# Splitting the normalised rows with the norm's weights alone, and applying the reciprocal root where products leave PSUM

## What is computed

```python
def rms_norm(x, g):
    x32 = x.astype(jnp.float32)
    y = x32 * lax.rsqrt(jnp.mean(x32 * x32, axis=-1, keepdims=True) + EPS)
    return (y * g.astype(jnp.float32)).astype(x.dtype)

def swiglu_ffn(h, w_gate_up, w_down):
    gate, up = jnp.split(h @ w_gate_up, 2, axis=-1)
    return (jax.nn.silu(gate) * up) @ w_down
...
        x = x + y
        x = x + swiglu_ffn(rms_norm(x, norm_ffn[i]), w_gate_up[i], w_down[i])
...
    kv = rms_norm(x, norm_kv) @ w_kv
...
    s = jnp.einsum('...qkgd,...ckd->...kgqc', q, k, preferred_element_type=jnp.float32) * ATTN_SCALE
```

## Time and profile before

| | us |
|---|---|
| median of 3 runs (3222.97 to 3225.34) | 3224.47 |
| the profiled execution | 3223.44 |
| its span, first to last instruction | 3221.6 |
| PE matmul busy | 3057.3 |
| DVE busy | 1764.2 |
| ACT busy | 1380.2 |
| POOL busy | 244.7 |

### The profile page before, as it was taken

The page is one execution under the profiler, slowest core; times in us unless marked ns, Lnnn a source line. Parts: engine busy times, 40 slices in busy tenths (PEclk is TensorE's granted clock), DMA queues, the critical chain, the costliest instruction groups (busy, mean ns, idle before and its releaser), DMA issues.

```text
span 3221.6 us, 72232 instructions
## 1 busy us (share of the span) xinstructions
PE 3057.3 (95%) x27157; PEld 2946.7 (91%) x27157; DVE 1764.2 (55%) x2676; ACT 1380.2 (43%) x2035; POOL 244.7 (8%) x295
## 2 busy tenths in 40 slices
PE   5899999999999998999999999879989999999998
PEld 3899999999998898999999999868888999999997
DVE  2577677677676545544444444556545444444444
ACT  3455455454454333444444333345534444443333
POOL 0111111111121001100000000120002000000000
PEclk8999999999999999999999999989999999999999
DMA  7545545545544454555555555534345555555553
GB/s 212 152 136 161 150 137 160 148 140 155 150 143 151 154 173 148 166 181 180 179 181 177 177 174 177 162 115 132 112 150 157 179 179 181 178 182 175 179 172 130
DMA packets 514689, 519.06 MB, mean 161 GB/s; under 512 B 30876, under 2 KB 437541, under 8 KB 513893
## 3 DMA queue, kind: packets, MB, share of 16 engines
q1 hardware_dynamic: 505490, 498.85, 50.0%
q0 software_dynamic: 2128, 13.69, 1.3%
q10 hardware_dynamic: 6866, 3.50, 0.4%
HBM read 491.99 MB, written 32.82 MB: 163 GB/s over the span
## 4 chain that ended last, share of the span: by engine, by line
PE 86%; DVE 7%; issue 3%; ACT 2%; DMA 1%; SPq 0%; DVEq 0%; ACTq 0%; POOLq 0%
PE bank L442 26%; PE bank L443 24%; PE bank L444 24%; PE bank L1619 4%; DVE norm_h L579 1%; DVE s_dec L2079 1%; DVE w_lo L430 1%; DVE h_lo L595 1%; ACT w_hi L423 1%; PE bank L1757 0%; PE bank L1804 0%; PE bank L1646 0%; DVE x_res L2125 0%; DMA hcol<-in_dt_bias_dram 0%; PE bank L962 0%
## 5 line engine op out<-in xcount | busy, mean ns | idle before, releaser
L430 DVE TENSOR_TENSOR w_lo<-w_raw,w_hi 128x1024 fp32r<-128x1024 f32 x830 | 1015.0, 1224 | 1042.8 <-ACT w_hi L423 1042.5
L423 ACT ACTIVATE w_hi<-w_raw 128x1024 fp32r<-128x1024 f32 x858 | 907.3, 1058 | 1408.4 <-PE bank L444 1399.2
L442 PE MATMUL bank<-h_hi,w_hi 128*128 128x264 f32 x4624 | 1368.3, 296 | 51.5 <-DVE w_lo L430 20.5
L443 PE MATMUL bank<-h_lo,w_hi 128*128 128x264 f32 x4624 | 1319.9, 285 | 0.0
L444 PE MATMUL bank<-h_hi,w_lo 128*128 128x264 f32 x4624 | 1319.4, 285 | 0.0
L442 PEld LDWEIGHTS bank<-h_hi,w_hi 128*128 128x128 f32 x4624 | 878.1, 190 | 79.2 <-issue 43.8
L443 PEld LDWEIGHTS bank<-h_lo,w_hi 128*128 128x128 f32 x4624 | 879.6, 190 | 1.7
L444 PEld LDWEIGHTS bank<-h_hi,w_lo 128*128 128x128 f32 x4624 | 877.8, 190 | 0.0
L442 PE MATMUL bank<-a_hi,w_hi 128*128 128x264 f32 x1408 | 402.1, 286 | 7.7 <-DVE x_res L2125 4.5
L443 PE MATMUL bank<-a_lo,w_hi 128*128 128x264 f32 x1408 | 402.8, 286 | 0.0
L444 PE MATMUL bank<-a_hi,w_lo 128*128 128x264 f32 x1408 | 402.1, 286 | 0.0
(11 more groups left out here) (352 smaller groups left out, 2950.3 us busy)
## 6 DMA issues: line engine op xcount, KB each, us to landing
w_raw<-in_w_gate_up_dram SPq DMA_DIRECT2D x704, 256.0 KB, 2.9
w_raw<-in_w_in_a_dram SPq DMA_DIRECT2D x388, 256.0 KB, 3.0
w_raw<-in_w_down_dram SPq DMA_DIRECT2D x352, 256.0 KB, 2.9
w_raw<-in_w_out_a_dram SPq DMA_DIRECT2D x128, 256.0 KB, 2.9
w_raw<-in_w_q_b_dram SPq DMA_DIRECT2D x64, 256.0 KB, 3.1
w_raw<-in_w_o_b_dram SPq DMA_DIRECT2D x64, 256.0 KB, 2.9
s_dec<-in_state_delta_dram SPq DMA_DIRECT2D x30, 512.0 KB, 5.2
out_dram<-s_dec SPq DMA_DIRECT2D x28, 512.0 KB, 4.7
```

The source lines that it names most:

```text
L423: nc.scalar.activation(w_hi[:, s % SPL, :], w_raw[:, s, :], ACT.Copy).then_inc(hi_ready, 1)
L430: ops.tensor_tensor(w_lo[:, s % SPL, :], w_raw[:, s, :], w_hi[:, s % SPL, :].bitcast(F32), ALU.subtract).then_inc(lo_ready, 1)
L442: nc.tensor.matmul(bank[bk][:, 0:T], wh, xh, start=first, stop=False)
L443: nc.tensor.matmul(bank[bk][:, 0:T], wh, xl, start=False, stop=False)
```

## The change

The hi and lo parts of the FFNs', keys' and queries' input are now made of x*gain without rstd, four tiles at a time, as soon as a unit of x_res is added: `hi_unit` on ACT, `lo_unit` on DVE, in slots 0 and 1 of the next unit, with the square in slot 1 and its sums in slot 2 (`unit_act`, `unit_dve`). The last unit's parts are made in the first three slots of the next stage. `norm_pe` now stands ahead of the next stage's chunk 5, into bank 4, and `norm_act` after ACT's slot 5. The root is applied later: in the FFN, DVE multiplies each of the four banks by rstd as it leaves PSUM (`scaled`), ACT takes silu of the two scaled gates in SBUF, DVE multiplies (`hidden`), ACT rounds, DVE takes the rest, in slots 0 to 2; keys and values are scaled in `keys_values_out`; queries are not, and the scores take the root as a factor for each row (rs_col, turned by three transposes). GpSimd makes no w_lo any more. `add_columns` and ACT's `columns` are written out; PE's loops stay. The FFN loop's tail moves into down's first three slots.

The core of the diff:

```diff
-        def scale_pair(dve, which, j):
-            n, g = NORMS[which][0:2]
-            after(dve, pair_lo, PAIRS * n + j)
-            for t in (2 * j, 2 * j + 1):
-                m = nc.vector.scalar_tensor_tensor(norm_h[:, t % 2, :], x_res[:, t, :],
-                                                   gains[:, g * KT + t:g * KT + t + 1], rstd[:, :], ALU.mult, ALU.mult)
-            m.then_inc(pair_scaled, 1)
...
+        def hi_unit(act, which, n):
+            k, g = STAGE[which], GAIN[which] * KT
+            act.wait_ge(u_read, UNITS_SQUARED[k] + n + 1)
+            if which == "kv" and n < 3:
+                act.wait_ge(w_used, C_DOWN[0] + 3 * UNIT["down"] + 16)
+            for t in range(4 * n, 4 * n + 4):
+                m = nc.scalar.activation(gained(which)[0][:, t, :], x_res[:, t, :], ACT.Copy, scale=gains[:, g + t:g + t + 1])
+            m.then_inc(unit_hi, 1)
+        def lo_unit(dve, which, n):
+            g = GAIN[which] * KT
+            hi, lo = gained(which)
+            dve.wait_ge(unit_hi, split_count(which, n))
+            for t in range(4 * n, 4 * n + 4):
+                m = nc.vector.scalar_tensor_tensor(lo[:, t, :], x_res[:, t, :], gains[:, g + t:g + t + 1],
+                                                   hi[:, t, :].bitcast(F32), ALU.mult, ALU.subtract)
+            m.then_inc(unit_lo, 1)
...
+        def unit_act(act, k, n, slot):
+            last = k == 1 and n == 3
+            if slot == 0 and k < 3:
+                hi_unit(act, "kv" if last else BEFORE[k], n)
+            elif slot == 1:
+                square_unit(act, k, n)
+            elif slot == 2 and last:
+                hi_unit(act, "mix1", 3)
...
-            first_splits(C_GU[0], PAIRS)
-            first_splits(C_KV, UNIT["kv"] + 4)
...
-                def silu(n, u):
-                    act.wait_ge(w_used, per * n + (C_GU[l] + per))
-                    act.wait_ge(u_read, n + U_GU[l])
-                    for t in range(2):
-                        m = nc.scalar.activation(f_silu[:, t, :], bank[4 * u + t][:, 0:T], ACT.Silu)
-                    m.then_inc(f_silued, 1)
-                def hidden_hi(n):
-                    act.wait_ge(u_read, n + (U_GU[l] + 1))
-                    nc.scalar.activation(a_hi[:, ds(2 * n, 2), :], f_h[:, :, :], ACT.Copy).then_inc(f_hi, 1)
                 def once(i, first=False):
                     for j in range(2 * per):
                         split_hi(act, chunk(C_GU[l], 2 * per, i, j + 1))
-                        if first and j + 1 < PAIRS:
-                            hi_pair(act, f"ffn{l}", j + 1)
-                        if j == 0 and not first:
-                            silu(2 * i - 1, 1)
-                        elif j == 1 and not first:
-                            hidden_hi(2 * i - 1)
+                        if first and j < 3:
+                            unit_act(act, 2 * l, 3, j)
+                        elif first and j == 5:
+                            norm_act(act, f"ffn{l}", 4)
...
+            def columns_out():
+                act.wait_ge(cols_turned, 1)
+                nc.scalar.activation(rs_col[:, 0:2], bank[5][:, 0:2 * P:P], ACT.Copy, scale=ATT).then_inc(cols_out, 1)
+                nc.scalar.activation(rs_col[0:HP, 2:3], bank[5][0:HP, 2 * P:2 * P + 1], ACT.Copy).then_inc(cols_out, 1)
             def kv_out():
-                act.wait_ge(w_used, C_Q)
-                for n in range(2):
-                    nc.scalar.activation(kvT[:, n, :], bank[4 + n][:, 0:T], ACT.Copy).then_inc(k_out, 1)
+                act.wait_ge(k_out, 2)
                 for n in range(2):
                     for h in range(2):
-                        m = nc.scalar.activation(kswap[HD * h:HD * (h + 1), n, :],
-                                                 bank[4 + n][HD * (1 - h):HD * (2 - h), 0:NP], ACT.Copy)
-                m.then_inc(u_read, 1)
+                        nc.scalar.activation(kswap[HD * h:HD * (h + 1), n, :],
+                                             kvT[HD * (1 - h):HD * (2 - h), n, 0:NP], ACT.Copy)
...
+                        if first and j == 5:
+                            norm_pe(pe, f"ffn{l}", 4)
                         if k == 0:
                             pe.wait_ge(u_read, 2 * i + (U_GU[l] + u - 1))
-                        if first and j < PAIRS:
-                            pe.wait_ge(pair_lo, PAIRS * NORMS[f"ffn{l}"][0] + j + 1)
+                        if first and j == UNIT["gu"]:
+                            pe.wait_ge(norm_ln, 2 * l + 2)
...
+            def add_unit(base, per, u):
+                dve.wait_ge(w_used, base + per * (u + 1))
+                for n in range(4):
+                    x = x_res[:, 4 * u + n, :]
+                    m = tt(x, x, bank[4 * (u % 2) + n][:, 0:T], ALU.add)
+                m.then_inc(u_read, 1)
+            def add_columns(base, per, k, last=False, done=0):
+                for j in range(done, 4 * per):
+                    u, slot = divmod(j, per)
+                    if not (last and j == 4 * per - 1):
+                        split_lo(dve, chunk(base, RAW, 0, j + 1))
+                    if k in (1, 3) and j == 0:
+                        scaled(k // 2, FT // 2 - 1, 1)
+                    elif k in (1, 3) and j == 1:
+                        hidden(k // 2, FT // 2 - 1)
+                    elif k in (1, 3) and j == 2:
+                        hidden_lo(k // 2, FT // 2 - 1)
+                    if u:
+                        unit_dve(dve, k, u - 1, slot)
+                    if k == 1 and u == 3 and 18 <= slot < 21:
+                        lo_unit(dve, "kv", slot - 18)
+                    if slot == per - 1:
+                        if k == 0 and u == 0:
+                            dve.wait_ge(x_back, 16)
+                        add_unit(base, per, u)
+            f_up = norm_h
...
+            def scaled(l, n, u):
+                dve.wait_ge(w_used, UNIT["gu"] * n + (C_GU[l] + UNIT["gu"]))
+                for t in range(2):
+                    m = tt(f_gate[:, t, :], bank[4 * u + t][:, 0:T], rstd[:, :], ALU.mult)
+                m.then_inc(gate_scaled, 1)
+                for t in range(2):
+                    m = tt(f_up[:, t, :], bank[4 * u + 2 + t][:, 0:T], rstd[:, :], ALU.mult)
+                m.then_inc(u_read, 1)
...
+            def hidden(l, n):
+                dve.wait_ge(f_silued, n + (FT // 2 * l + 1))
+                dve.wait_ge(u_read, n + (U_GU[l] + 1))
+                tt(f_h[:, :, :], f_gate[:, :, :], f_up[:, :, :], ALU.mult).then_inc(f_mult, 1)
+            def hidden_lo(l, n):
+                dve.wait_ge(f_hi, n + (FT // 2 * l + 1))
+                tt(a_lo[:, ds(2 * n, 2), :], f_h[:, :, :], a_hi[:, ds(2 * n, 2), :].bitcast(F32),
+                   ALU.subtract).then_inc(f_lo, 1)
...
+            def keys_values_out():
+                dve.wait_ge(norm_rstd, 3)
                 dve.wait_ge(w_used, C_Q)
-                for n in range(2):
-                    nc.vector.tensor_copy(kvT[:, 2 + n, :], bank[6 + n][:, 0:T]).then_inc(v_out, 1)
+                for n in range(4):
+                    m = tt(kvT[:, n, :], bank[n][:, 0:T], rstd[:, :], ALU.mult)
+                    if n < 2:
+                        m.then_inc(k_out, 1)
+                m.then_inc(u_read, 1)
...
-                    stt(scores_sb[:, p, h, 0:256], s[:, 0:256], ATT, b, ALU.mult, ALU.add).then_inc(p_add, 1)
-                    stt(scores_sb[:, p, h, 256:384], s[:, 256:384], ATT, b[:, 128:256], ALU.mult, ALU.add
+                    stt(scores_sb[:, p, h, 0:256], s[:, 0:256], rs_col[:, 1:2], b, ALU.mult, ALU.add).then_inc(p_add, 1)
```

More of the change, by code:

```diff
@@ L370, in yoco_step @@
         k_out = sem("k_out")
-        v_out = sem("v_out")
         bias_in = sem("bias_in")
@@ L551, in norm_pe @@
             for u in range(4):
                 pe.wait_ge(part_ready, 4 * k + u + 1)
[L553 removed]
+                m = nc.tensor.matmul(bank[bk][:, 0:T], ones, part[:, u, :], start=(u == 0), stop=(u == 3))
             m.then_inc(norm_added, 1)
[L556 to L563 removed]
@@ new lines, in unit_act, with unit_dve @@
+        def unit_act(act, k, n, slot):
[6 more added lines that the diff above has]
+                hi_unit(act, "mix1", 3)
+        def unit_dve(dve, k, n, slot):
+            last = k == 1 and n == 3
+            if slot == 1 and k < 3:
+                lo_unit(dve, "kv" if last else BEFORE[k], n)
+            elif slot == 2:
+                part_unit(dve, k, n)
+            elif slot == 3 and last:
+                lo_unit(dve, "mix1", 3)
@@ L2159, in once @@
-                        if first and j + 1 < PAIRS:
-                            scale_pair(dve, which, j + 1)
-                        if j == 0 and not first:
-                            hidden(2 * i - 1, 1)
-                        elif j == 1 and not first:
-                            hidden_lo(2 * i - 1)
+                        split_lo(dve, chunk(C_GU[l], 2 * per, i, j + 1))
+                        if first and j < 3:
```

(11 more changed lines are left out.)

263 lines of the change are left out of this document (107 added, 156 removed).

## The result

The changed kernel takes **3187.36 us** (median of 4 runs, 3182.53 to 3191.76) against 3224.36 (3222.97 to 3225.34): a ratio of 0.9885, interval 0.9868 to 0.9902. That is 37 us less; 3194 had been forecast, with 3166 to 3214. The profiled execution of the changed kernel took 3191.76 with a span of 3190.0, 31.6 us under the span of before.

A forecast was written before the change was run, and what follows sets the result against it. PE was taken as the bound, busy 3057 of 3222 us. 3223.44 less gains of 88.5 plus 58.5 added gave 3193.4 us for the profiled execution, 3194 for the median, with a range of 3166 to 3214.

The forecast's parts named there:

- FFN handovers: From OUT's or down's end to chunk 8 of each FFN: PE's norm wait mostly goes, gaining 18.9 and 18.6 us.
- KV and Q's first round: From the stage's start to first queries out: 85.75 us shrinks to 44.5, gain 39.5 after a 1.7 clock allowance.
- the price of the transposes: In KV and Q's first round: 26 and three new transposes stay, at 1.05 us for four, 7.6 us.
- Squares at odd units: Square waits a slot later: OUT and O gain 3.85 us each, 7.7 in all; down stages given nothing.
- The FFN unit: Waits between ACT and DVE add 1.33 us of PE idle a unit, 58.5 us for 44 units.
- The first stall: In an FFN unit ahead of chunk 2: silu waits for DVE's scaled gates, 0.64 us of PE idle.
- the second: In an FFN unit ahead of chunk 3: the rounding waits for DVE's product, 0.70 us of PE idle.
- Tail of the loop: At two down starts: the FFN loop's last steps stop costing 1.9 us each, gain 3.8 us.
- Queries: Stretch from first queries out to O's first add: no change forecast, 0 us.
- Hidden handovers: Rival: FFN silu and rounding find slack, wholly (3136 us) or in part (3164 us); chance 0.12 for 3136 to 3170.
- The slower rival: Clock falls at the new FFN stalls, 1.4 us each, 44 falls 63 us: 3257 us; chance 0.10 for 3210 to 3260.

The follow-up runs named there:

- experiment 7: Experiment 1's kernel again, 3135.47 us, and the same with PE's two down stages written out without their loop, 3124.16 us.
- Experiment 1: Changed kernel with silu and the gate-up product one slot later, the rounding and its rest two slots later: 3132.5 us, ratio 0.9721.
- shifted versions: Changed kernel with silu, product, rounding and rest moved to later slots, with PE's down loop kept (3132.5, 3135.47 us) or written out (3124.16 us).
- experiment 5: Changed kernel with one more ACT copy of 1056 columns behind each silu of an FFN unit: 3227.26 us, ratio 1.0006 to the kernel before.

## Why the prediction was right, point by point

- **FFN handovers** (18.9 and 18.6): 25.2 us for eight chunks in both layers, a gain of 19.0 and 18.7. The two microseconds that were left for a late first split and the sum over partitions are there.
- **KV and Q's first round** (39.5): 44.8, and the term is too small by 5.3. The new length was put at 44.5 plus 1.7 for a clock that may fall; it is 40.9 at a clock of 1.00. Of the 5.3, 1.7 is that allowance. The rest is mainly the price of the transposes: I took 1.05 us for four from the earlier trace rows, a row that ran at a granted clock of 0.50. In the changed kernel four take 0.60:

```profile
2096.39 0.60 PE L935 MATMUL bank<-masks,k_win 127*128 127x127 f32 x4
```

  For 29 of them that is 4.4 us and not 7.6. A duration from a stretch at a low clock was carried into one at full clock.
- **Squares at odd units** (3.85 each): 3.9 and 4.0. In the down stages nothing was promised and the profile has +1.1 and -1.4; experiment 7 shows that the turn of PE's loop is all there is.
- **The FFN unit** (1.33 us, 58.5): the mechanism is as told, wait by wait, and the sum is 5.9 us too high. Experiment 1 gives 1.20 a unit, 52.6 in all. The first stall was mis-sized: by PE's starts 0.55 us and not 0.64, since ACT's late split starts 3.59 us after the one before it (the unit above) and not 3.70; the second is 0.68 for 0.70. The two rows of DVE's scalings above, 24.61 us apart against 23.29, would have confirmed 1.33 falsely: units alternate, as the engines' loop holds two of them. Over all 21 intervals of the first FFN the mean is 24.57; before it is 23.37 (23.28 and 23.46 in turn) without the first and the last interval, whose steps stand elsewhere.
- **Tail of the loop** (1.9 a layer): from chunk 8 to down's first add the stages are 24.2 and 24.4 longer; 26.3 for the units leaves 2.0 for the tail.
- **Queries** (nothing): the profiled execution has +9.0, another of the same kernel +5.0, and four profiles of the shifted versions +3.1 to +9.0. This is the term that failed. I took a stretch with unchanged waits to be unchanged; its clock wasn't.
- **Sum**: -5.3 in KV and -5.9 in the units against +9.0 in the queries and +2.1 in unchanged work ahead of OUT. The forecast of 3193.4 for the profiled execution met 3191.8 because misses of both signs nearly cancel, and one of them, the queries' 9.0, varies between executions of the same code: so close a hit is luck. The terms are good to some 6 us each, and without the queries' 9 us the forecast would have been some 10 too high. The median is 6.6 below the forecast, since the profiled execution is the slowest of the four.

**The rivals.** Hidden handovers: refuted, the waits are there and go away with experiment 1. The slower rival, that the clock falls at the new stalls: refuted for these, by 1.00 in both FFNs (1300 to 1780 and 2430 to 2900 us) and by experiment 5. The Trainium skill (TensorE: Matmul & The Clock Gate, section A second HAM failure mode: psum-queue depth-cycling) has micro-idles between groups of matmuls, if frequent enough, set off such falls. Here 0.24 and 0.44 us in each 24.6, and 1.22 and 0.39 in each 25.5, were not enough; in the queries' stretch, where single waits are up to 2.4 us long, the clock did fall 2 to 12 times. The share of idle time doesn't tell the two apart: PE is busy for 94% of the queries' stretch before and for 93% of experiment 5's FFN. The rival had the right effect in the wrong place.

## What to carry to other kernels

Taking a norm's root off the path by linearity is worth its whole handover, 19 us ahead of an FFN and 45 at the keys here, the old norm's contention with GpSimd included, but each new dependence between two engines that share the split of the weights must be given a slot of room: the same work one or two slots later was 55 us faster. Count where each waiting step stands in its engine's queue and what is queued behind it; the arithmetic of ends and starts was good to 11%. Take durations of PE only from rows at the clock you expect, and measure a period over many turns.

## What the runs showed of the hardware

- The queries' stretch, the same matmuls (1482 in most traces) with waits alike, took from 181.7 to 197.8 us in thirteen profiles, by the number of falls of the granted clock (2 to 12, each 1.7 us). The falls come in patterns that recur to 0.2 us, in different kernels too. Unaltered code gave 186.6 and 190.6 in two executions, and a copy of 1.09 us ahead of it 13 us more. A gain elsewhere can be given back in such a stretch, or seem larger than it is.
- DVE's scaling of two tiles takes 3.01 us beside GpSimd's split (2.40) and 0.89 without it. That contention was on the norm's chain; giving the split to DVE (1.23 us a chunk) cost as much as it saved.
- A stall of 1.2 us in every 25 us left the clock at 1.00; a turn of PE's loop with 2.6 us of idle was followed by 0.55 for 3.2 us, and 14 of 18 such turns by a fall. Writing the loop out gave 2.2 to 5.6 us a stage.
- An idle of 0.24 us between two overlapping matmuls is a delay of 0.50 us: 0.16 of it is overlap lost, and 0.10 the late start of the second matmul behind it.
